# Stationary probabilities for the sample values, and an earlier load of the convolution's parameters, in a hybrid RWKV-7 and sparse-attention decoder layer

## What is computed

```python
def decoder_layer(x, pos, shift_prev, wkv_prev, conv_prev, attend, lw):
    n = rmsnorm(x, norm1)
    c_rw, c_att, c_gate = _split(n @ w_in, (RW_COLS, ATT_COLS, GATE_COLS))
    o_rw, wkv_new, shift_new = rwkv7_mix(c_rw, ...)
    ...
    o_att = attend(q, k, v, qi, ki, wi * IDX_W_SCALE)
    merged = sigmoid(g_rw) * (o_rw @ p_rw) + sigmoid(g_att) * (o_att @ p_att)
    h = x + merged @ w_o
    f, conv_new = conv_glu(rmsnorm(h, norm2), conv_prev, w_up, conv_w, conv_b, w_down)
    return h + f, ...

def sparse_attend(q, kg, vg, valid):          # per request: 8 heads, 2 key/value heads of 128
    s = einsum('bqgrd,bqkgd->bqgrk', qg, kg) * HEAD_DIM ** -0.5
    p = softmax(where(valid, s, -inf))
    o = einsum('bqgrk,bqkgd->bqgrd', p, vg)   # the product the change rewrites, for the samples

def conv_glu(n, conv_prev, w_up, conv_w, conv_b, w_down):
    gate, up = _split(n @ w_up, (D_FF, D_FF))
    ext = concatenate([conv_prev, gate], axis=1)
    c = conv_b + sum_j ext[:, j:j + T] * conv_w[j]       # j = 0, 1, 2
    return (silu(c) * up) @ w_down, ext[:, T:]
```

## Time and profile before

| | |
|---|---|
| median of 3 runs | 1928.93 us (1928.53 to 1933.64) |
| profiled execution, its own time | 1924.94 us |
| its span in the trace | 1923.4 us |
| PE busy | 1849.6 us, 96% |
| DVE, ACT, POOL busy | 59%, 36%, 9% |
| chain that ended last | PE 80%, DVE 12%, ACT 3%, issue 2% |
| sample products L716 and L718, 96 records | 338.4 to 346.5 us and 422.9 to 432.9 us |
| w_up stage begins | 1060.9 us |

### The profile page before, as it was taken

How to read it: one execution, slowest core, us unless ns; L and a number is a source line. 1 busy time by engine, 2 the same in 40 slices (tenths; PEclk the granted TensorE clock), 3 DMA queues, 4 the chain that set the end, 5 groups by cost and what they waited for, 6 DMA issues and landing times.

```text
span 1923.4 us, 41121 instructions
## 1 busy us (share of the span) xinstructions
PE 1849.6 (96%) x16744; PEld 1759.5 (91%) x16744; DVE 1132.4 (59%) x2015; ACT 700.5 (36%) x910; POOL 168.0 (9%) x126
## 2 busy tenths in 40 slices
PE   5999989999999999999999999999999999999997
PEld 3999858998888888889999999999999999999997
DVE  4333866217777777776655666666666666344444
ACT  4333234333333333343334433333333333333332
POOL 2600325441000000000000000000000000000000
PEclk7999989999999999999999999999999999999998
DMA  4644323331222222245444544444444444544443
GB/s 180 220 162 166 110 102 110 125 139 62 103 103 103 92 92 103 99 148 175 172 154 169 218 162 166 169 158 165 162 172 155 167 160 161 209 164 164 160 162 135
DMA packets 50746, 283.49 MB, mean 147 GB/s; under 512 B 7104, under 2 KB 12160, under 8 KB 24576
## 3 DMA queue, kind: packets, MB, share of 16 engines
q1 hardware_dynamic: 43488, 260.87, 39.2%
q10 hardware_dynamic: 3072, 12.63, 1.7%
q0 software_dynamic: 4128, 9.18, 1.4%
HBM read 274.38 MB, written 8.27 MB: 147 GB/s over the span
## 4 chain that ended last, share of the span: by engine, by line
PE 80%; DVE 12%; ACT 3%; issue 2%; DMA 1%; POOL 1%; DVEq 0%; ACTq 0%; SPq 0%
PE bank L575 25%; PE bank L577 23%; PE bank L576 23%; DVE w_lo L524 1%; PE bank L907 1%; PE bank L873 1%; POOL w_lo L524 1%; DVE w_lo L532 1%; DVE squares_k L1753 1%; DVE x_raw L1555 1%; DVE y_sq L1938 1%; ACT w_hi L540 1%; DVE rope_tmp L1593 1%; DMA w_raw<-in_w_down 1%; PE bank L716 1%
## 5 line engine op out<-in xcount | busy, mean ns | idle before, releaser
L575 PE MATMUL bank<-x_split,w_lo 128*128 128x288 f32 x2944 | 907.0, 308 | 22.4 <-DVE x_split L1561 16.6
L576 PE MATMUL bank<-x_split,w_hi 128*128 128x288 f32 x2944 | 873.3, 297 | 0.0
L577 PE MATMUL bank<-x_split,w_hi 128*128 128x288 f32 x2944 | 870.7, 296 | 0.0
L540 ACT ACTIVATE w_hi<-w_raw 128x2048 fp32r<-128x2048 f32 (+1 forms) x264 | 472.4, 1789 | 573.4 <-PE bank L577 554.5
L524 DVE TENSOR_TENSOR w_lo<-w_raw,w_hi 128x2048 fp32r<-128x2048 f32 (+1 forms) x215 | 451.1, 2098 | 311.2 <-ACT w_hi L540 311.2
L575 PEld LDWEIGHTS bank<-x_split,w_lo 128*128 128x128 f32 x2944 | 556.3, 189 | 49.3 <-issue 29.8
L576 PEld LDWEIGHTS bank<-x_split,w_hi 128*128 128x128 f32 x2944 | 557.4, 189 | 4.2 <-issue 0.7
L577 PEld LDWEIGHTS bank<-x_split,w_hi 128*128 128x128 f32 x2944 | 558.5, 190 | 0.0
L575 PE MATMUL bank<-act_split,w_lo 128*128 128x288 f32 x704 | 208.9, 297 | 1.0 <-DVE w_lo L524 1.0
L576 PE MATMUL bank<-act_split,w_hi 128*128 128x288 f32 x704 | 207.9, 295 | 0.0
L577 PE MATMUL bank<-act_split,w_hi 128*128 128x288 f32 x704 | 207.3, 294 | 0.0
(11 more groups left out here) (366 smaller groups left out, 1602.5 us busy)
## 6 DMA issues: line engine op xcount, KB each, us to landing
w_raw<-in_w_up SPq DMA_DIRECT2D x88, 1024.0 KB, 4.8
w_raw<-in_w_in SPq DMA_DIRECT2D x48, 1024.0 KB, 4.9
w_raw<-in_w_down SPq DMA_DIRECT2D x64, 704.0 KB, 4.0
w_raw<-in_w_gate SPq DMA_DIRECT2D x32, 1024.0 KB, 4.8
w_raw<-in_w_p SPq DMA_DIRECT2D x16, 1024.0 KB, 4.8
w_raw<-in_w_o SPq DMA_DIRECT2D x16, 1024.0 KB, 4.8
x_raw<-in_x SPq DMA_DIRECT2D x4, 576.0 KB, 6.4
h<-in_x ACTq DMA_DIRECT2D x1, 2304.0 KB, 10.4
```

Source lines behind the costliest of these rows:

```text
L540: actv(WHI[:, slot, 0:kt], WRAW[:, slot, 0:kt], ACT.Copy).then_inc(sem("w_hi"), 1)
L575: mm(out, wl, hi, start=first and k == ks[0], stop=False, skip_group_check=True)
L576: mm(out, w, lo, start=False, stop=False, skip_group_check=True)
L577: ins = mm(out, w, hi, start=False, stop=last and k == ks[-1], skip_group_check=True)
```

## The change

In the products of the sample values the sides are exchanged: 32 columns of probabilities (8 heads by 4 tokens of one request) are the stationary side, and the request's values for both key/value heads, 256 columns, move. The four requests of a half write to four strips of 32 partitions of bank 6. ACT copies the 128x256 result to prob_t (`pv_sb`), TensorE transposes it in two steps into bank 7, and ACT copies from there the part that belongs to each head. Between the product and the transposes stand 4 fill blocks (FILL_PV). Second, the two loads of the convolution's parameters are issued after the first four w_o units, once `merged` is complete, and the wait for `h_spilled` moves from DVE's first convolution step to ACT, before its first write of the gated products.

```diff
-FILL_ROPE, FILL_TOPK_S, FILL_DOTS, FILL_TOPK, FILL_SCORES, FILL_SOFTMAX, FILL_P_T = 4, 24, 2, 64, 8, 9, 10
+FILL_ROPE, FILL_TOPK_S, FILL_DOTS, FILL_TOPK, FILL_SCORES, FILL_SOFTMAX, FILL_P_T, FILL_PV = 4, 24, 2, 64, 8, 9, 10, 4
...
                 if n:
                     pe.wait_ge(sem("o_sb"), n)
+                for kc in range(2):
+                    for b in range(4):
+                        c0 = kc * P + 32 * b
+                        mm(BK[6][32 * b:32 * b + 32, 0:KVH * HDIM], PRT[:, c0:c0 + 32], VC[:, b, kc, :], start=kc == 0, stop=False,
+                           skip_group_check=True)
                 for b in range(4):
-                    for g in range(KVH):
-                        out = BK[6][:, (b * KVH + g) * 16:(b * KVH + g + 1) * 16]
-                        c0 = b * 32 + g * 16
-                        for kc in range(2):
-                            mm(out, VC[:, b, kc, g * P:(g + 1) * P], PRT[:, kc * P + c0:kc * P + c0 + 16],
-                               start=kc == 0, stop=False)
-                        ins = mm(out, VNEW[:, b, g * P:(g + 1) * P], PRT[0:DS, 2 * P + c0:2 * P + c0 + 16],
-                                 start=False, stop=True)
+                    c0 = 2 * P + 32 * b
+                    ins = mm(BK[6][32 * b:32 * b + 32, 0:KVH * HDIM], PRT[0:DS, c0:c0 + 32], VNEW[:, b, :], start=False, stop=True,
+                             skip_group_check=True)
+                ins.then_inc(sem("pv_tok"), 1)
+                fill_cols(FILL_PV)
+                pe.wait_ge(sem("pv_sb"), half + 1)
+                for g in range(KVH):
+                    ins = tr(BK[7][:, g * P:(g + 1) * P], PRT[:, 512 + g * P:512 + (g + 1) * P], ident)
                 ins.then_inc(sem("pv"), 1)
...
                 filled(FILL_P_T)
+                if kind == "sample":
+                    act.wait_ge(sem("pv_tok"), which + 1)
+                    actv(PRT[:, 512:512 + KVH * HDIM], BK[6][:, 0:KVH * HDIM], ACT.Copy).then_inc(sem("pv_sb"), 1)
+                    filled(FILL_PV)
                 act.wait_ge(sem("pv"), n + 1)
                 if kind == "sample":
                     c0 = SEQ + 16 * which
-                    for b in range(4):
-                        ins = actv(COLS[:, T_Q:T_Q + AH, c0 + DS * b:c0 + DS * b + DS],
-                                   BK[6][:, b * 32:b * 32 + 32].rearrange("p (h t) -> p h t", t=DS), ACT.Copy)
+                    for g in range(KVH):
+                        own = BK[7][:, g * P:(g + 1) * P].rearrange("p (b g h t) -> p b g h t", b=4, g=KVH, t=DS)[:, :, g]
+                        q = COLS[:, T_Q + 4 * g:T_Q + 4 * g + 4, c0:c0 + 16].rearrange("p h (b t) -> p b h t", t=DS)
+                        ins = actv(q, own, ACT.Copy)
                     ins.then_inc(sem("o_sb"), 1)
...
             o_units(0)
+            act.wait_ge(sem("merged"), KT)
+            act.dma_start(CPREV[:], a["conv_prev"]).then_inc(sem("cprev_in"), 16)
+            act.dma_start(CONVP[:], a["conv_params"]).then_inc(sem("convp_in"), 16)
             with act.Fori(1, D_GROUPS) as g:
                 o_units(g)
             act.wait_ge(sem("h_sum"), KT)
             act.dma_start(h_spill, H[:].rearrange("p k n -> p (k n)")).then_inc(sem("h_spilled"), 16)
-            act.dma_start(CPREV[:], a["conv_prev"]).then_inc(sem("cprev_in"), 16)
-            act.dma_start(CONVP[:], a["conv_params"]).then_inc(sem("convp_in"), 16)
             norm_root(1, HRSTD)
...
                     act.wait_ge(sem("up_out"), g * 2 + (j + 1))
+                    if isinstance(g, int) and j == 0:
+                        act.wait_ge(sem("h_spilled"), 16)
...
             norm_rstd(1, HRSTD)
-            dve.wait_ge(sem("h_spilled"), 16)
-            dve.wait_ge(sem("x_split"), 4 + KT)
             dve.wait_ge(sem("cprev_in"), 16)
             dve.wait_ge(sem("convp_in"), 16)
```

## The result

The changed kernel takes 1911.42 us (median of 4 runs, 1910.11 to 1911.85), the kernel before 1928.93 in the three runs shown, and 1928.55 in the 91 runs of it that stand beside the experiments below. A fourth run of the kernel before, beside the changed one, took 5055.87 us; it is left out, and nothing shows why it was so long. The ratio is 0.990, 95% interval 0.988 to 0.992. The forecast was 1917.5 with a range from 1912.5: right in direction, 6 us too slow, and outside its range by 1 us. For the profiled execution it was 1913.5, and that took 1911.25.

What follows compares the result with a forecast made beforehand. TensorE was taken as the bound, except in a tail set by ACT and DVE. Terms -9.86 - 10.10 + 2 x 2.4 + 3.2 + 1.2 - 0.6 = -11.4 us gave a median of 1917.5 us, range 1912.5 to 1923.5.

Steps and rivals of the forecast that it cites:

- What bounds the kernel: TensorE paces until 433.04 (fill block worth 0.40 us); then ACT and DVE for 19.6 us, the tail, where blocks are free.
- Removed products: Old sample products: half 0 saves 9.86 us (8.09 plus 1.77 slow-clock fill), half 1 saves 10.10.
- Added products: New sample products on four overlapping strips: 2.0 us a half, plus 0.4 for transposes, clock staying at 1.00.
- (a): Rival: the four strips do not overlap, 4.7 us instead of 1.7 a half; 1923.5 us, chance 0.08.
- (d): Rival: strips do not overlap and the new products do not hold the clock; +6.5 us, 1935.4, chance 0.03.
- The new wait: TensorE's wait for ACT's 128x256 copy before the transposes: hidden by four fill blocks, 0.6 us without them.
- The moved blocks: Eight fill blocks move from the tail into the two halves, where TensorE sets the pace: +3.2 us.
- The split before half 1: TensorE reaches POOL's split earlier and waits 1.7 us for it instead of 0.5: +1.2 us.
- Rival (c): More late splits (2 us) and slow clock behind the tail (up to 1.7 us): -7.7, 1921.2 us, chance 0.11.
- The convolution: Parameters loaded early, so DVE's weight split is on time and TensorE's wait at 1075.60 goes: -0.6 us.
- the forecast's own bounds: 1.3 to 3.1 us for a half's products and 0 to 2 us for the split: 1915.5 to 1920.5 us.
- the last one of the sum: The -11.4 us, 1913.5 for the profiled execution, was carried to the 1928.93 median, 4.0 above it: 1917.5 us.

Runs made afterwards that it cites:

- b_late8: Kernel before with four more fill blocks ahead of each sample half's old products and eight fewer in the tail; 1933.76 us, ratio 1.0027.
- pv0: Changed kernel with FILL_PV = 0, no fill between new products and transposes, the eight blocks back in the tail; 1907.59 us.
- b_cut: Kernel before with only eight of the 24 sample products a half (keys 0 to 127 alone); 1911.40 us.
- a_late13: Changed kernel with 17 superfluous 256-column products ahead of each half's new products, to put everything behind about as late as before; 1929.78 us.
- late13_pieces: a_late13 with h read back from h_spill in four loads of 576 KB; 1930.26 us.
- conv_only: Kernel before with only the convolution's part of the change, sample products as before; 1927.27 us, ratio 0.9989.
- a_again: The changed kernel unaltered, run once more beside the others; 1910.93 us, ratio 0.9904.

## Why the prediction was wrong

By its steps:

- **What bounds the kernel: right.** The tail is 19.54 us where it was 19.58, a block is worth 0.40 before it and little in it: eight fewer save nothing in b_late8, eight more cost 0.9 us in pv0.
- **Removed products: right, at the short end.** They were read from an execution in which half 0 took 8.09 us; in five others with the old products in full it was 8.2 to 9.4.
- **Added products: the mechanism right, the size 0.4 us a half too high** (1.57 against 2.0), the transposes 0.2 (0.4 said, 0.2 found). The clock stayed up, as said; (a) and (d) fall with it. The estimate of 1.5 us a half, from the 2.38 of the Trainium skill's page TensorE: Matmul & The Clock Gate, Part 3, was nearer than my 2.0.
- **The new wait: right in size** (0.5 us and a change in pv0), and hidden. That ACT has nothing else due there is wrong for half 0: a unit ends in its four fill blocks, and the weights' copy (L540, 1.92 us at 339.73) puts the copy of the result off to 341.54. No wait of TensorE comes of it.
- **The moved blocks, +3.2: right. The split before half 1: 1.28 us, 1.7 said**, and 0.33 before, where I had 0.5. Rival (c)'s slow clock behind the tail is there (0.50 from 434 to 444) and costs 0.3 to 0.4 us at the first pair between the two profiles; over five of each kind it averages out to nothing.
- **The convolution: 0.6 said, 0.9 to 1.3 found.** The wait of TensorE that I summed (0.62 at 1075.60) was not all: the units behind it were late by as much again.

These come to 12.0 us in the sample stage and 1.1 in the convolution, against 10.8 and 0.6. That is 1.7 us of the 6, and would have been inside the range. (The lower end of the forecast's own bounds, 1915.5, should be 1914.9 by its terms: 1.4 for the products and 1.2 for the split.)

**The step that failed is the last one of the sum: "I predict for the median: 1917.5", the same 11.4 taken from a number that lay 4.0 above the profiled execution.** It takes what separates the median from that execution for something the change leaves alone. It does not. What separates them lies in places behind or in the changed code:

- The moment at which the clock falls in the old products: 113.7 to 115.5 us for the sample stage in five traces, 114.2 in the profiled one.
- The w_down weights beside the read back of h: 1.0 us of wait in the first profile; 3.0, 3.1 and 2.8 in three others with its loads.
- More time at the lower clock in the longer runs. At 1924.94 the profiled execution had a mean granted clock of 0.984, where 69 of the 91 runs have 0.983 or less. Part of it is the first place again, an earlier fall in the old products; where the longest runs have theirs, no trace shows.

The profiled execution was near the low end: only 3 of the 91 runs lie below its 1924.94. The changed kernel is near its low end most of the time (9 runs, 1910.11 to 1911.85), so at the median it gains the difference as well. By the experiments about 2.8 us of the gap are the w_down weights: four traces of before's kind stand 3.2 us above the shortest, six of the changed kind 0.4, and at the median the four small loads give 3.3 us before and 0.5 after. The last 1.6 us (17.5 less 12.0, 1.1 and 2.8) stand in no trace. That they are clock is argued and not shown: among the 91 runs those at 0.984 or more have a median 2 us below that of all.

**What stays open** is why the w_down weights and the clock cost the kernel before more, beyond its old products. That the moment matters, at which a stage comes, is argued and not shown. For it speaks that a delay of 6 us costs 6 and one of 15 costs 19 at the median, and that b_cut, with the old code at the new time, has a wait of 0.2; but b_cut's runs scatter up to 1922.20, and a_late13's wait for w_down, 0.8, is no longer than that of the changed kernel's first profile, 1.3. The rival is that the added instructions themselves do it: a_late13 and late13_pieces have 34 more products, and both stop at the same matmul with no wait that the profile shows. No run delays TensorE by 15 us without adding to its program.

## What to carry to other kernels

Before a forecast is moved from the profiled execution to the median, ask where the difference between them lies: rows with a DMA-bound wait or with a clock that falls in mid-stage are the ones that vary, and a change that shifts or removes them takes the excess along. A second profile of the same kernel, or the spread of its runs (1924 to 1936 here against 1910 to 1912 after), tells more of that than any further row of the first. And a cover of fill in front of a short wait has a price: eight blocks at 0.40 us hid two waits of 0.5.

## What the hardware showed

- Four strips of 32 columns, 128 rows each and 256 columns moving, give eight f32 products in 1.00 to 1.02 us in either order, and in 3.57 us on one strip.
- Beside a POOL tensor_tensor of 4.5 us a DVE scalar_tensor_tensor with two inputs in SBUF, whose record starts 0.05 us before it, took 4.88 us; with POOL's instruction held back it took 0.48.
- With 1728 KB of h on another queue ACT waited 7.6 us for the next 704 KB of weights in conv_only, and 4.1 us in a_again.
- The last pair's chunk inversion (32x32 products) ran at a clock of 0.60 over 12 us in the trace of a_late13 and at 1.00 in that of late13_pieces, with the same instructions ahead of it.
- Among runs of one kernel, a mean granted clock that was lower by 0.003 went with 4.5 us (the two heaps of late13_pieces) to 5.4 us (the kernel before).
